# RWKV pairs of a three-block transformer kernel: the rate product behind the solved products, and the dense passes of four head pairs dealt as one sequence

## The reference

```python
w_log = -softplus(-(w0 + tanh(wd) @ w2)) - 0.5
decay = exp(-exp(w_log))
a = sigmoid(a0 + ad @ a2)                       # the rate
kk = k * k_k, each head scaled to length 1
k = k * (1.0 + (a - 1.0) * k_a)                 # the key with its rate product
def step(S, (r, w, k, v, -kk, kk * a)):         # one token, S is 64x64 for each of 8 heads
    S = S * w + (S @ a_t) b_t^T + v k^T
    return S, S @ r
bonus = sum(r * k * r_k) * v                    # per head, added behind the group norm
```

## Time and profile before

| what | value |
|---|---|
| median of 3 runs | 2545.0 us (2543.87 to 2549.95) |
| the profiled execution | 2545.44 us, its span 2543.6 us, granted clock 0.997 |
| TensorE busy | 2502.6 us, 98% |
| VectorE busy | 1315.8 us, 52% |
| ScalarE busy | 698.2 us, 27% |
| GpSimd busy | 1511.3 us, 59% |
| chain that ended last | TensorE 90%, VectorE 5% |

### The profile page before, as it was taken

One profiled execution on the slowest core, in us unless ns is written; L12 is line 12 of the kernel. 1 busy time (PEld: TensorE's weight loads), 2 busy tenths in 40 slices (PEclk: granted clock), 3 DMA queues, 4 the chain that ended last, 5 costly groups with the idle time before them and its releaser, 6 DMA issues.

```text
span 2543.6 us, 46931 instructions
## 1 busy us (share of the span) xinstructions
PE 2502.6 (98%) x16248; PEld 2017.2 (79%) x16248; DVE 1315.8 (52%) x1981; ACT 698.2 (27%) x1306; POOL 1511.3 (59%) x963
## 2 busy tenths in 40 slices
PE   8989999999999999999999999999999999999999
PEld 6868888887877778888888888877778878888887
DVE  7866556465566657664322224566657753322224
ACT  4452000024135446522100002135446521100002
POOL 5666666656645455556666666645455556666665
PEclk9999999999999999999999999999999999999999
DMA  4213222223211132223222223211132223222223
GB/s 167 72 42 116 95 99 92 98 87 117 91 52 52 44 100 71 75 79 103 99 93 96 99 94 118 93 50 52 44 100 75 72 78 103 91 99 97 93 99 100
DMA packets 72442, 222.55 MB, mean 87 GB/s; under 512 B 9312, under 2 KB 12256, under 8 KB 72288
## 3 DMA queue, kind: packets, MB, share of 16 engines
q1 hardware_dynamic: 71856, 220.36, 26.1%
q10 hardware_dynamic: 432, 0.14, 0.0%
HBM read 218.37 MB, written 2.10 MB: 87 GB/s over the span
## 4 chain that ended last, share of the span: by engine, by line
PE 90%; DVE 5%; DVEq 2%; issue 1%; DMA 1%; POOL 1%; ACT 1%; ACTq 0%; POOLq 0%; SPq 0%
PE acc L551 79%; PE bank L551 10%; DMA raw<-in_w_pg 1%; DVE rw_kp L1742 1%; PE bank L1223 0%; POOL w_lo L377 0%; DVE y_lo L1261 0%; DVEq L1718 0%; DVE bank L1261 0%; DVE sumsq L1261 0%; DVE xg_lo L1654 0%; DMA vec<-in_vec 0%; POOL w_hi L370 0%; PE bank L994 0%; DVE bank L1620 0%
## 5 line engine op out<-in xcount | busy, mean ns | idle before, releaser
L377 POOL TENSOR_TENSOR w_lo<-raw,w_hi 128x1024 fp32r<-128x1024 f32 (+3 forms) x438 | 961.7, 2196 | 300.4 <-PE acc L551 258.1
L370 POOL TENSOR_SCALAR w_hi<-raw 128x1024 fp32r<-128x1024 f32 (+3 forms) x438 | 436.4, 996 | 598.9 <-PE acc L551 515.2
L551 PE MATMUL acc<-xg_hi,w_hi 128*128 128x512 f32 x2208 | 579.8, 397 | 8.3 <-DVE xg_lo L1354 3.7
L551 PE MATMUL acc<-xg_lo,w_hi 128*128 128x512 f32 x2208 | 568.6, 393 | 0.0
L551 PE MATMUL acc<-xg_hi,w_lo 128*128 128x512 f32 x2208 | 564.9, 393 | 0.3 <-POOL w_lo L377 0.3
L551 PEld LDWEIGHTS acc<-xg_hi,w_hi 128*128 128x128 f32 x2208 | 410.2, 188 | 108.9 <-issue 24.0
L551 PEld LDWEIGHTS acc<-xg_hi,w_lo 128*128 128x128 f32 x2208 | 411.6, 188 | 87.6 <-issue 1.5
L551 PEld LDWEIGHTS acc<-xg_lo,w_hi 128*128 128x128 f32 x2208 | 412.2, 188 | 86.4 <-DVE xg_lo L1654 0.7
L2139 ACT ACTIVATE ffn_act<-ffn_t 128x512 f32<-128x512 f32 x100 | 63.2, 632 | 744.8 <-DVEq L1321 600.7
L1261 DVE TENSOR_TENSOR x<-x,acc 128x512 f32<-128x512 f32 x104 | 71.4, 687 | 311.5 <-PE acc L551 311.0
L1261 DVE TENSOR_TENSOR bank<-acc,rstd 128x512 f32<-128x512 f32 x72 | 50.4, 700 | 260.8 <-PE acc L551 260.7
(11 more groups left out here) (352 smaller groups left out, 2716.4 us busy)
## 6 DMA issues: line engine op xcount, KB each, us to landing
raw<-in_w_up SPq DMA_DIRECT2D x132, 512.0 KB, 3.2
raw<-in_w_down SPq DMA_DIRECT2D x48, 512.0 KB, 3.2
raw<-in_w_gate SPq DMA_DIRECT2D x48, 512.0 KB, 3.2
raw<-in_w_ret SPq DMA_DIRECT2D x32, 512.0 KB, 3.3
raw<-in_w_rw SPq DMA_DIRECT2D x28, 512.0 KB, 3.2
raw<-in_w_o SPq DMA_DIRECT2D x48, 256.0 KB, 2.6
raw<-in_w_in SPq DMA_DIRECT2D x18, 512.0 KB, 3.3
raw<-in_w_down SPq DMA_DIRECT2D x24, 384.0 KB, 3.0
```

Of the source, the lines that this page charges most:

```text
L370: nc.gpsimd.tensor_scalar(w_hi[:, s, 0:n], raw[:, s, 0:n], 1.0, 0.0, ALU.mult, ALU.add).then_inc(w_half[s], 1)
L377: nc.gpsimd.tensor_tensor(w_lo[:, s, 0:n], raw[:, s, 0:n], bits(w_hi[:, s, 0:n]), ALU.subtract).then_inc(w_split[s], 1)
L551: return nc.tensor.matmul(o, a, b, start=first, stop=last, skip_group_check=shared)
```

## The change

Two things change, both in the RWKV pairs. VectorE's steps of `decays` stand elsewhere: step 4 leaves level 4 and comes behind the eviction of AU, after step 2; steps 5 and 6 leave that place and come behind `qev`, that is behind the first state's copy and the update of AR. And the dense passes are dealt as one sequence over the four pairs, 100, 96, 96 and 92, with new numbers for pair 0 and a row of its own for pair 3. A slot is then begun before its pair is over; the assertion at the pair's end compares the running count.

```diff
-                FILLS = ((23, 9, 1, 5, 3, 5, 3, 5, 4, 5, 6, 4, 4, 2, 2, 2, 3, 4, 3, 3),
-                         (4, 10, 3, 6, 5, 6, 4, 6, 1, 6, 7, 8, 5, 3, 2, 3, 4, 5, 4, 4))
+                FILLS = ((24, 8, 3, 4, 3, 4, 3, 5, 4, 7, 8, 5, 4, 2, 2, 2, 3, 3, 3, 3),
+                         (4, 10, 3, 6, 5, 6, 4, 6, 1, 6, 7, 8, 5, 3, 2, 3, 4, 5, 4, 4),
+                         (4, 10, 3, 6, 5, 6, 4, 6, 1, 6, 7, 8, 5, 3, 3, 3, 3, 3, 3, 3))
+                STREAM = (0, sum(FILLS[0]), sum(FILLS[0]) + sum(FILLS[1]), sum(FILLS[0]) + 2 * sum(FILLS[1]), 4 * 96)
...
-                    fills = iter(FILLS[min(j, 1)])
-                    passes = 0
+                    fills = iter(FILLS[(0, 1, 1, 2)[j]])
+                    passes = STREAM[j]
...
-                            part(s % 2, F + s // 2, lo, lo + n)
+                            part(s % 2, I + s // 2, lo, lo + n)
...
-                    assert passes == 96
+                    assert passes == STREAM[j + 1]
...
-                        elif lev == 4 and j < 3:
-                            decays(j + 1, 4)
                     after("au", j, 1, 1)
                     v.tensor_copy(rw["AU"][:, 1].rearrange("p n s t -> p (n s t)"), bank[1][:])
                     say("auev")
                     if j < 3:
-                        for step in (2, 5, 6):
+                        for step in (2, 4):
                             decays(j + 1, step)
...
                     say("qev")
+                    if j < 3:
+                        for step in (5, 6):
+                            decays(j + 1, step)
```

More of the change, by code:

```diff
@@ L924, in variance @@
                     mm(bank[5 if j == 3 else 1][:], K["g2"][:, j, :], z_rw[:, 13, :], True, True).then_inc(s2["gate"], 1)
-                FILLS = ((23, 9, 1, 5, 3, 5, 3, 5, 4, 5, 6, 4, 4, 2, 2, 2, 3, 4, 3, 3),
-                         (4, 10, 3, 6, 5, 6, 4, 6, 1, 6, 7, 8, 5, 3, 2, 3, 4, 5, 4, 4))
+                FILLS = ((24, 8, 3, 4, 3, 4, 3, 5, 4, 7, 8, 5, 4, 2, 2, 2, 3, 3, 3, 3),
+                         (4, 10, 3, 6, 5, 6, 4, 6, 1, 6, 7, 8, 5, 3, 2, 3, 4, 5, 4, 4),
+                         (4, 10, 3, 6, 5, 6, 4, 6, 1, 6, 7, 8, 5, 3, 3, 3, 3, 3, 3, 3))
+                STREAM = (0, sum(FILLS[0]), sum(FILLS[0]) + sum(FILLS[1]), sum(FILLS[0]) + 2 * sum(FILLS[1]), 4 * 96)
+                assert STREAM[3] + sum(FILLS[2]) == STREAM[4]
                 def state_products(j):
@@ L938, in rwkv_pair @@
                 def rwkv_pair(j):
-                    F = I + 2 * j
                     G, X, Y, AU, AW, SCB, SCK = (rw[k] for k in ("G", "X", "Y", "AU", "AW", "SCB", "SCK"))
                     R = 1 + j % 2
-                    fills = iter(FILLS[min(j, 1)])
-                    passes = 0
+                    fills = iter(FILLS[(0, 1, 1, 2)[j]])
+                    passes = STREAM[j]
                     def fill():
```

## The result

| | median | against the kernel before (ratio, 95% interval) |
|---|---|---|
| before, the runs taken beside the changed kernel's | 2546.32 us | |
| changed kernel | 2551.13 us | 1.0025 [1.0018, 1.0033], about 6.4 us slower |
| predicted | 2549.7 us (2540.0 to 2554.0) | 4.7 us slower |

The kernel is slower, by 4.8 us between the medians and by 6.4 us by the ratio. The time is in the predicted range. The profiled span is 2547.6 us, 4.0 over before's.

A forecast was written before the change was run, and what follows sets the result against it. TensorE, busy 98% of the span, was taken as the bound, so only its pauses could change. The terms -3.8, -2.2 and +11.3 - 0.6 summed to +4.7 us on the 2545.0 us median: 2549.7 us, range 2540 to 2554.

The forecast's parts named there:

- step 3: Key product and bon behind qev: GpSimd holds both up, TensorE's sums start late; +11.3 us, 0.6 us back.
- Rival A: VectorE is not held up behind qev, which costs only 1.2 us; 2539.6 us in all; chance 0.13.
- rival B: Behind qev VectorE is held up once, by x * z_rt; bon precedes high_part; cost 7.2 us, total 2545.6; chance 0.13.
- Step 1: Rate product leaves level 4: the 0.95 us pause at level 5 goes in pairs 1 and 2, both layers; -3.8 us.
- rival C: At level 5 AU stays where it was, waiting for the previous pair's gated product; -3.8 us lost, 2553.5 us; chance 0.10.
- Step 2: New dealing of passes: pair 0 0.2 us shorter, pair 3's chain 0.9 us shorter, per layer; -2.2 us in both.

The follow-up runs named there:

- places alone: Kernel before with only the decays steps moved as in the change, old dealing of 96 passes per pair; 2552.0 us, ratio 1.0024.
- high_part late: Changed kernel with GpSimd's high_part made to wait until bon is written; 2545.4 us, ratio 1.0000.
- x * z_rt early: Changed kernel with GpSimd's x * z_rt moved straight behind the fifth mask, without the wait for the first state; 2542.1 us, ratio 0.9985.
- all steps behind AU: Changed kernel with decays steps 2, 4, 5, 6 behind AU's eviction: 2542.7 us, 0.9990; same places on the kernel before, old dealing: 2542.2 us, 0.9985.

## Why the prediction was right, and where it was off

*The mechanism of step 3* is shown. The predicted times in pair 1 were 798.57 for the end of the key product, 800.07 for `bon` and 800.27 for the sums; they are 798.49, 799.93 and 800.11. In distances: from the first product of T and S to the sums of `bon` it is 0.16 us where nothing waits and 800.11 - 798.05 = 2.06 here, 1.90 late, where 1.95 was forecast. In pair 2 it is the same, in pair 0 751.31 - 749.75 - 0.16 = 1.40 where 1.75 was forecast. In layer 1 it is 1.65, 1.51 and 1.90. That makes 10.3 us for 11.3. Rival A needed 0.69 and 0.75 us, rival B 0.75 for `bon`: both are out. Some of it is given back behind the sums, where 0.6 us was forecast: from the sums to the last products of AR and S, places alone takes 8.20, 8.42 and 8.52 us in pairs 0, 1 and 2 of layer 0, the kernel before 8.38, 8.53 and 8.71. That is 0.5 us, and 0.6 in layer 1, together 1.0. It comes in all three pairs, not at pair 0's third round alone. Trading one GpSimd instruction away at a time (high_part late, x * z_rt early) shows each half.

*Step 1* was right in size if it is the only change: the pause of 0.95 us goes, and AU is not late for another reason, which puts rival C out. In pair 1 the level 5 stretch is 1.82 us. But as a term of this sum it was double work, since the dealing by itself removes it. The forecast read `low_part`'s start as fixed; its own row had the releaser, the passes of acc.

*Step 2* is the term that failed: it took the dealing for a gain of its own, 2.2 us. Beside a rate product already moved, the comparison of the kernels with all steps behind AU shows none (0.9990 and 0.9985), and in the profiles layer 0's pairs are 0.25 us shorter and layer 1's 0.40 longer. Pair 0's pauses at level 5 are filled, 0.42 and 0.43 us in the earlier trace rows and none at 737.04 and 739.91, which just pays for the four passes: in these two kernels pair 0 is 0.17 us longer with them in layer 0 and 0.52 in layer 1, where 0.2 shorter was forecast. Pair 3's chain did shrink as forecast, from 7.0 to 901.50 - 895.37 = 6.13 us; but ahead of it, among the products SCK by tokV, TensorE now idles 0.88 us with no releaser, where before had 0.25 ahead of the passes, and pair 3 of layer 0 is no shorter; in layer 1 nothing stands at this place and it is 0.48 us shorter. All kernels with the new dealing have the pause there in layer 0, 0.59 to 1.14 us.

The traces give a hint at what this pause is: it ends at 894.31, 1.40 us after a packet of the queue that the profile calls `instruction` (891.60 to 892.91, 16 KB), and so do all 56 pauses without a releaser of 0.4 us or more in the pairs of the thirteen profiles, 1.2 to 1.6 us after the end of such a packet, where these come about every 8 us. That TensorE waits there for its own instructions is argued from this, not tested.

A further 0.30 and 0.18 us at the boundaries of the pairs, from the last state products to the next pair's first, are also new with the dealing (1.17 and 1.05 us for 0.87), and open.

*The sum*: with the parts as measured it is -3.8 for the pause, 0 for the dealing, +10.3 for the waits and -1.0 given back, +5.5 us, for 6.4 of the ratio, whose interval reaches from 4.6 to 8.4. The forecast of 4.7 lies inside it because errors cancelled: step 2 was counted for 2.2 us that did not come, and step 3, net, for 10.7 where the parts give 9.3. The pairs of the profiles, 6.5 us longer, hold 1.4 us of the lower clock and the pauses at the boundaries, which the forecast did not have; 0.7 and 1.6 us of the 2.5 gained outside the pairs are the pause at 940.21 and the lower clock at 2067.25 of the one profile before. That the number is within 2 us of the measured one is in part luck; the direction is not, it hangs on the held steps.

The Trainium skill ("SBUF — State Buffer", "Who interferes with whom") says that the order of issue, not the operation, decides who blocks. These runs agree, with numbers for the lead: 0.03 us (scan, 3.42 for 1.23 us) and 0.05 us were enough for GpSimd, 0.14 us for VectorE. It also names `tensor_scalar` among the operations that can contend in a two-port mode, though it has one input; the rate product is one, and was held to 2.33 us.

## What to carry to other kernels

Before a VectorE instruction with two SBUF inputs is moved into idle time, look at what GpSimd issues there: the idle time counts only for the stretch in which GpSimd's queue is empty, and with two such steps in a row each can meet another GpSimd instruction. Two edits that aim at one pause do not add; ask of each whether the other already moves the engine that causes it. A start that hangs on another engine's progress (here GpSimd's on the dense passes) moves with every edit to that engine, so an order that is good with one dealing can be bad with the next.

## What the runs showed that was not expected

- A lead of 0.03 to 0.14 us decides a difference of 2 us for VectorE against 0.2 us for GpSimd: losing costs the loser the length of the other's instruction, and GpSimd's are the long ones.
- Pauses of TensorE that the profile gives no releaser, 0.15 to 1.4 us each, add up to 3.6 us over both layers' pairs before and to 3.8 to 6.1 in the other kernels, mostly among the small products. They are of the size of the effects studied here. The long ones all end 1.2 to 1.6 us after an instruction packet.
- The profiles of two kernels can differ by a stretch at the lower clock, about 1.5 us, that one has at a place where the other has none. Before two spans are compared, look for it: here it hid in 6.5 us of loss and in 2.5 us of gain.
